# Decode attention: a group's scores behind the transposes of the next key page, with a ring of three PSUM banks

## The chip, the cores and the metric

One core of a Trainium2 chip runs the kernel once. The metric is the device time in microseconds of that one core. A profiled execution stands beside the timed runs; its rows are times from the start of its span.

## What is computed

One layer of a decoder for a prompt of 512 tokens and 8 requests ("sample group") of 4 new tokens each. The part at hand is the differential attention of the 8 requests over 1024 cached keys and values:

```python
s = jnp.einsum('bqhmd,bkhmd->bhmqk', q, k, preferred_element_type=jnp.float32) * (DA_HEAD_DIM ** -0.5)
...
s = jnp.where(causal, s + bias[:, None], -jnp.inf)
p = jax.nn.softmax(s, axis=-1)
a = p[:, :, 0] - lam * p[:, :, 1]
return jnp.einsum('bhqk,bkhd->bqhd', a, v)
```

There are 8 heads, two softmax maps per head and 4 queries, so 64 score rows for a request. Keys and values lie in a cache of pages of 128 keys, 512 KB each, found through a page table: 8 key pages and 8 value pages for a request. Feed-forward blocks, projections, the prompt's attention and a retention branch stand before and behind this stage and are not touched.

## The kernel before, in words

Each engine has its own program, and they meet at semaphores. All five programs of the stage are unrolled over requests b = 0 to 7 and pages g = 0 to 7 except SyncE's, which loops over the middle requests. `DecodeAttention` (from line 1140) holds them. Products are made in two parts: each float operand is split in a "high" part (a rounding copy to the matmul type) by ScalarE and a "low" part (source less high) by VectorE.

A key page lands in one of four slots of `k_page`. `turn` (line 1255) transposes it on TensorE in two halves of four heads: half 0 goes to PSUM bank 0 and half 1 to bank 1. Before each half it waits until the low part of the half two earlier is taken (`kT_lo`, line 1260). ScalarE's `act_key` writes the high half to `kt_hi`, VectorE's `dve_key` the low one to `kt_lo` (`key_half`, line 1374). `kt_hi` and `kt_lo` have two slots of two pages each, so ScalarE waits at an even page for the scores of the pair two earlier (`scored`, line 1386). `score_pair` (line 1266) multiplies two pages (a pair, q = 0 to 3) with the queries: one matmul for the bias and 16 for eight heads and two parts. It waits for both pages' low halves, for q = 0 also for the minimum taken of the request before (`s_min`) and the queries that GpSimd sets.

After the fourth pair of a request ScalarE copies the low score rows out (`act_low_rows`), VectorE adds the rest and takes the minimum (`dve_min`), ScalarE makes the exponential (`act_exp`), TensorE turns p (`turn_p`, line 1284, into bank 5), and ScalarE and VectorE split it (`act_p`, `dve_p`) into `pT`. Then the value pages: `act_value` and `dve_value` (lines 1395 and 1400) split a page into `vp_hi` and `vp_lo`, which have two slots, so page g waits for the matmuls of page g - 2 (`pv`). `values` (line 1298) makes four matmuls of a page into banks 6 and 7, and `values_new` (line 1309) adds the new tokens. ScalarE copies the output to `o_rows` (`act_keep`), VectorE prepares weights (`dve_weigh`), and `merge` (line 1315) makes 8 small fp32 matmuls (16 in the profile) out of it.

The order of the work is written out by hand, once for each engine: `pe_step` (line 1325), `act_step` (line 1447), `dve_step` (line 1534), and `sp_step` and `sp_ahead` (lines 1186 and 1200) for the loads on SyncE's queue. An engine takes its instructions in that order, and one that waits holds what is behind it. In the step of request b TensorE turns and scores the keys of b, multiplies the values of b - 1 (pages 0 to 5) and those of b - 2 (pages 6 and 7), and merges b - 2. Before, its order is: turn 0, values 6, turn 1, values 7 and new, turn 2, turn p, score 0, turn 3, values 0 and 1, score 1, merge, turn 4, values 2, turn 5, values 3, score 2, turn 6, values 4, turn 7, values 5, score 3. ScalarE and VectorE take value page g - 2 ahead of key page g for g = 4 to 7, and value pages 6 and 7 at the end of the step:

```python
for g in range(4, PAGES):
    if past:
        self.act_value(act, b - 1, g - 2)
    self.act_key(act, b, g)
```

A key page's load (`load_page`, line 1173) waits until the page four earlier is transposed, a value page's until the low part of the page four earlier is taken. Behind the last request a tail (lines 1359 to 1371) finishes the values of requests 6 and 7, with the first chunks of the next stage's gate between.

Of the kernel before, what the change touches and what calls it, by code (L numbers as in the profile page):

```python
# [15 lines left out]
P = 128  # L16
# [84 lines left out]
def build(nc, x_prompt, x_sample, cache_k, cache_v, state_ret, page_table, ln_g, ln_b, ffn1_w_gu,  # L101
# [6 lines left out]
    with ExitStack() as ctx:  # L108
# [1031 lines left out]
        class DecodeAttention:  # L1140
            def __init__(self):
# [29 lines left out]
                self.oa_set = sem("da_oa_set")  # L1171

# [13 lines left out]
            def sp_step(self, sp, b, older=True):  # L1186

                self.load_k(sp, b, 4)
                if older:
                    self.load_v(sp, b - 1, 2)  # L1190
                self.load_k(sp, b, 5)
                if older:
                    self.load_v(sp, b - 1, 3)
                self.load_k(sp, b, 6)
                self.load_k(sp, b, 7)
                if older:
                    self.load_v(sp, b - 1, 4)
                    self.load_v(sp, b - 1, 5)

            def sp_ahead(self, sp, b, older=True):  # L1200

                for g in range(2):
                    self.load_k(sp, b + 1, g)
                    if older:
                        self.load_v(sp, b - 1, 6 + g)
                for g in range(2):
                    self.load_k(sp, b + 1, 2 + g)
                    self.load_v(sp, b, g)

            def sp_part(self, sp):  # L1210
# [9 lines left out]
                self.sp_step(sp, DEC - 1)  # L1220
                self.load_v(sp, DEC - 2, 6)
# [33 lines left out]
            def turn(self, pe, b, g):  # L1255

                for half in range(2):
                    if half == 0:
                        pe.wait_ge(self.k_landed[g % 4], 32 * b + 16 * (g // 4) + 16)
                    pe.wait_ge(self.kT_lo, 16 * b + 2 * g + half + 1)  # L1260
                    for h in range(4):
                        mm = nc.tensor.transpose(ps[:, half, h * P:h * P + P],  # L1262
                                                 k_page[:, g % 4, (4 * half + h) * P:(4 * half + h) * P + P], ident[:])
# [20 lines left out]
            def turn_p(self, pe, b):  # L1284
                pe.wait_ge(self.exped, b + 1)
                pe.wait_ge(self.pT_lo, 2 * b + 2)

                nc.tensor.matmul(ps[:, 5, 0:ROWS], p_s[:, 0:P], ident[:, 0:ROWS], start=True, stop=True)
                for g in range(1, PAGES):
                    nc.tensor.transpose(ps[:, 5, ROWS * g:ROWS * g + ROWS], p_s[0:ROWS, P * g:P * g + P],  # L1290
# [34 lines left out]
            def pe_step(self, pe, b):  # L1325

                past, older = b >= 1, b >= 2
                self.turn(pe, b, 0)
                if older:
                    self.values(pe, b - 2, 6)  # L1330
# [5 lines left out]
                if past:  # L1336
                    self.turn_p(pe, b - 1)
                self.score_pair(pe, b, 0)
                self.turn(pe, b, 3)
                if past:  # L1340
                    self.values(pe, b - 1, 0)
                    self.values(pe, b - 1, 1)
                self.score_pair(pe, b, 1)
                if older:
                    self.merge(pe, b - 2)
                for q in (2, 3):
                    for g in (2 * q, 2 * q + 1):
                        self.turn(pe, b, g)
                        if past:
                            self.values(pe, b - 1, g - 2)  # L1350
                    self.score_pair(pe, b, q)

            def pe_part(self, pe):
# [3 lines left out]
                for b in range(DEC):  # L1357
                    self.pe_step(pe, b)
                self.values(pe, DEC - 2, 6)
# [14 lines left out]
            def key_half(self, b, g, half, hi):  # L1374
                src = ps[:, half, :].rearrange("p (h c) -> p h c", c=P)
# [29 lines left out]
            def p_parts(self):  # L1405

                return ((ps[:, 5, :].rearrange("p (g c) -> p g c", c=ROWS), pT[:, 0:PAGES, 0:ROWS],
# [28 lines left out]
            def act_p(self, act, b):  # L1436
                act.wait_ge(self.p_turned, b + 2)
                act.wait_ge(self.o_done, b + 1)
                for src, hi, _ in self.p_parts():
# [7 lines left out]
            def act_step(self, act, b):  # L1447
                past, older = b >= 1, b >= 2
                if past:
                    self.act_low_rows(act, b - 1)  # L1450
                self.act_key(act, b, 0)
                if past:
                    self.act_exp(act, b - 1)
                self.act_key(act, b, 1)
# [4 lines left out]
                self.act_key(act, b, 2)  # L1459
                if past:  # L1460
                    self.act_p(act, b - 1)
                    self.act_value(act, b - 1, 1)
                self.act_key(act, b, 3)
                for g in range(4, PAGES):
                    if past:
                        self.act_value(act, b - 1, g - 2)
                    self.act_key(act, b, g)
                if past:
                    self.act_value(act, b - 1, 6)
                    self.act_value(act, b - 1, 7)  # L1470

            def act_part(self, act):
                for b in range(DEC):
                    self.act_step(act, b)
                self.act_low_rows(act, DEC - 1)
                self.act_exp(act, DEC - 1)
# [41 lines left out]
            def dve_p(self, dve, b):  # L1518
                dve.wait_ge(self.pT_hi, 2 * b + 2)
                for src, hi, lo in self.p_parts():  # L1520
# [13 lines left out]
            def dve_step(self, dve, b):  # L1534
                past = b >= 1
                if past:
                    self.dve_min(dve, b - 1)
                self.dve_key(dve, b, 0)
                self.dve_key(dve, b, 1)
                if past:  # L1540
                    self.dve_value(dve, b - 1, 0)
                self.dve_key(dve, b, 2)
                if past:
                    self.dve_p(dve, b - 1)
                    self.dve_value(dve, b - 1, 1)
                self.dve_key(dve, b, 3)
                for g in range(4, PAGES):
                    if past:
                        self.dve_value(dve, b - 1, g - 2)
                    self.dve_key(dve, b, g)  # L1550
                    if past and g == 5:
                        self.dve_weigh(dve, b - 1)
                if past:
                    self.dve_value(dve, b - 1, 6)
                    self.dve_value(dve, b - 1, 7)

            def dve_part(self, dve):
                for b in range(DEC):
                    self.dve_step(dve, b)
                self.dve_min(dve, DEC - 1)  # L1560
                self.dve_value(dve, DEC - 1, 0)
# [656 lines left out]
```

## Time and profile before

| | us |
|---|---|
| median of 3 runs | 1928.66 |
| lowest, highest | 1927.82, 1928.72 |
| the profiled execution's own time | 1928.45 |
| its span | 1926.2 |
| TensorE busy in it | 1776.9 |
| VectorE, ScalarE busy in it | 780.3, 660.8 |
| first turn of the stage to its last merge | 736.23 to about 1020 |

PE is TensorE, PEld its weight loads, ACT ScalarE, DVE VectorE, POOL GpSimd and SPq SyncE's queue. A group of matmuls on one line is often folded into one row with its count (x8 is the eight transposes of one page). The span of 1926.2 us is what the rows cut up; the execution's own time lies 2.25 us over it. A number in square brackets is the idle time of the engine before the instruction, and what ended it.

### The profile page before, as it was taken

How to read it: one execution, taken by the hardware profiler on the slowest of the kernel's cores; microseconds unless marked ns; L12 is line 12 of the kernel's file. 1: busy time of each engine (PE TensorE's matmuls, PEld its weight loads, DVE VectorE, ACT ScalarE, POOL GpSimd, SP SyncE). 2: the span in 40 equal slices, each digit the busy share in tenths (PEclk: the TensorE clock that was granted, in tenths of full speed). 3: DMA queues.
4: the chain of work that ended last, by engine and by line, in shares of the span. 5: the costliest groups of instructions: out<-in, count | busy, mean ns of one | idle time of the engine just before them, and what ended most of it. 6: DMA issues, size and time to landing. Idle time of an engine off the chain costs nothing.

```text
span 1926.2 us, 32228 instructions
## 1 busy us (share of the span) xinstructions
PE 1776.9 (92%) x13095; PEld 1680.3 (87%) x13095; DVE 780.3 (41%) x1084; ACT 660.8 (34%) x867; POOL 97.1 (5%) x169
## 2 busy tenths in 40 slices
PE   5999999998998775889889999899999899999996
PEld 5999999987997545777778999769998899999996
DVE  2333332234223775676753222344345433333123
ACT  3333331124223554666744222124322433332111
POOL 0000000000002420000000000210000000000002
PEclk9999999998998898999979999999999999999998
DMA  4222222231431014788851232062222122222221
GB/s 140 88 87 87 87 87 98 82 92 39 134 122 36 1 34 145 260 279 276 274 186 44 87 100 88 31 199 72 95 87 97 37 88 89 89 88 84 84 98 46
DMA packets 146736, 204.12 MB, mean 106 GB/s; under 512 B 5538, under 2 KB 127330, under 8 KB 146658
## 3 DMA queue, kind: packets, MB, share of 16 engines
q1 hardware_dynamic: 145506, 198.55, 31.6%
q0 software_dynamic: 1152, 4.46, 0.6%
q8 instruction: 58, 0.95, 0.2%
q14 instruction: 20, 0.16, 0.0%
HBM read 191.59 MB, written 11.40 MB: 105 GB/s over the span
## 4 chain that ended last, share of the span: by engine, by line
PE 86%; DVE 6%; ACT 5%; issue 3%; DMA 0%; SPq 0%; POOL 0%; POOLq 0%; ACTq 0%; DVEq 0%
PE ps L297 68%; PE ps L1280 3%; PE ps L1305 2%; PE ps L1262 2%; PE ps L999 2%; DVE vp_lo L1402 2%; PE ps L311 1%; ACT vp_hi L1398 1%; PE ps L1013 1%; PE ps L636 1%; ACT kt_hi L1380 1%; PE ps L1708 1%; PE ps L1320 1%; PE ps L1700 1%; PE ps L721 1%
## 5 line engine op out<-in xcount | busy, mean ns | idle before, releaser
L297 PE MATMUL ps<-xh,w_hi_t 128*128 128x272 f32 x2368 | 495.8, 291 | 8.4 <-DVE xl L568 4.8
L297 PE MATMUL ps<-xl,w_hi_t 128*128 128x272 f32 x2368 | 491.9, 289 | 0.0
L297 PE MATMUL ps<-xh,w_lo_t 128*128 128x272 f32 x2368 | 490.6, 289 | 0.0
L283 DVE TENSOR_TENSOR w_lo_t<-w_raw,w_hi_t 128x2048 fp32r<-128x2048 f32 (+1 forms) x112 | 252.4, 2254 | 516.1 <-ACT w_hi_t L279 516.1
L297 PEld LDWEIGHTS ps<-xh,w_hi_t 128*128 128x128 f32 x2368 | 373.9, 190 | 10.7 <-issue 4.9
L297 PEld LDWEIGHTS ps<-xl,w_hi_t 128*128 128x128 f32 x2368 | 375.3, 190 | 0.0
L297 PEld LDWEIGHTS ps<-xh,w_lo_t 128*128 128x128 f32 x2368 | 373.2, 190 | 0.0
L279 ACT CAST w_hi_t<-w_raw 128x2048 fp32r<-128x2048 f32 (+1 forms) x112 | 209.9, 1874 | 277.1 <-PE ps L297 277.1
L297 PE MATMUL ps<-hh,w_hi_t 128*128 128x272 f32 x704 | 145.7, 288 | 0.0
L297 PE MATMUL ps<-hl,w_hi_t 128*128 128x272 f32 x704 | 145.4, 288 | 0.0
L297 PE MATMUL ps<-hh,w_lo_t 128*128 128x272 f32 x704 | 144.9, 287 | 0.0
L297 PEld LDWEIGHTS ps<-hl,w_hi_t 128*128 128x128 f32 x704 | 110.7, 189 | 0.0
L297 PEld LDWEIGHTS ps<-hh,w_hi_t 128*128 128x128 f32 x704 | 110.2, 188 | 0.0
L297 PEld LDWEIGHTS ps<-hh,w_lo_t 128*128 128x128 f32 x704 | 110.2, 188 | 0.0
L1381 DVE TENSOR_TENSOR kt_lo<-ps,kt_hi 128x512 fp32r<-128x512 f32 x128 | 82.6, 684 | 62.5 <-ACT kt_hi L1380 61.7
L399 ACT CAST hh<-prod 128x544 f32 x44 | 28.5, 648 | 214.8 <-DVE prod L416 214.8
L1380 ACT CAST kt_hi<-ps 128x512 fp32r<-128x512 f32 x128 | 70.1, 589 | 77.8 <-PE ps L1262 75.3
L1262 PE MATMUL ps<-ident,k_page 128*128 128x128 f32 x512 | 72.1, 284 | 20.5 <-DVE kt_lo L1381 18.1
L1262 PEld LDWEIGHTS ps<-ident,k_page 128*128 128x128 f32 x512 | 58.4, 145 | 33.8 <-issue 30.3
L1402 DVE TENSOR_TENSOR vp_lo<-v_page,vp_hi 128x1024 fp32r<-128x1024 f32 x64 | 78.2, 1223 | 21.0 <-ACT vp_hi L1398 17.9
L416 DVE TENSOR_TENSOR prod<-ps,gated 128x544 f32<-128x544 f32 x44 | 31.9, 725 | 107.0 <-PE ps L297 107.0
L1398 ACT CAST vp_hi<-v_page 128x1024 fp32r<-128x1024 f32 x64 | 67.3, 1053 | 20.1 <-PE ps L1305 20.1
(249 smaller groups left out, 2126.6 us busy)
## 6 DMA issues: line engine op xcount, KB each, us to landing
w_raw<-in_ffn_w_gu_dram SPq DMA_DIRECT2D x44, 1024.0 KB, 5.0
w_raw<-in_w_in_dram SPq DMA_DIRECT2D x32, 1024.0 KB, 5.7
k_page<-in_cache_k_dram SPq DMA_DIRECT2D x64, 512.0 KB, 4.3
v_page<-in_cache_v_dram SPq DMA_DIRECT2D x64, 512.0 KB, 4.6
w_raw<-in_ffn_w_down_dram SPq DMA_DIRECT2D x16, 1024.0 KB, 5.1
w_raw<-in_ffn_w_down_dram SPq DMA_DIRECT2D x8, 768.0 KB, 4.4
w_raw<-in_w_branch_a_dram SPq DMA_DIRECT2D x4, 1024.0 KB, 5.2
st_in<-in_state_ret_dram SPq DMA_DIRECT2D x8, 512.0 KB, 5.3
```

Of the source, the lines that this page charges most:

```text
L279: nc.scalar.copy(w_hi_t[:, j, 0:nk], w_raw[:, j, 0:nk]).then_inc(hi_split, 1)
L283: nc.vector.tensor_tensor(w_lo_t[:, j, 0:nk], w_raw[:, j, 0:nk], w_hi_t[:, j, 0:nk].bitcast(F32), ALU.subtract).then_inc(lo_split, 1)
L297: mm = nc.tensor.matmul(ps[:, bank + half, 0:HALF], w[:, j, k, w_cols], m[:, k0 + k, half * HALF:half * HALF + HALF], start=start and k == ...
L416: nc.vector.tensor_tensor(halves(prod[:, n]), banks(4 + 2 * n), halves(gated[:, n]), ALU.mult).then_inc(self.prod_done, 1)
L999: mm = nc.tensor.matmul(ps[:, 2 * s + m, 0:n], q_stage[:, s, m], kaT[:, h, 0:n], start=True, stop=True)
L1262: mm = nc.tensor.transpose(ps[:, half, h * P:h * P + P], k_page[:, g % 4, (4 * half + h) * P:(4 * half + h) * P + P], ident[:])
L1280: mm = nc.tensor.matmul(dst, q_stat[:, P * h:P * h + P], kt[:, q % 2, h, 0:n], start=False, stop=h == HA - 1 and kt is kt_lo)
L1305: mm = nc.tensor.matmul(ps[:, 6 + half, :], pT[:, g], v[:, g % 2, 512 * half:512 * half + 512], start=g == 0 and v is vp_hi, stop=False)
L1380: return nc.scalar.copy(at_hi, src)
L1381: return nc.vector.tensor_tensor(at_lo, src, at_hi.bitcast(F32), ALU.subtract)
L1398: nc.scalar.copy(vp_hi[:, g % 2], v_page[:, g % 4]).then_inc(self.v_hi, 1)
L1402: nc.vector.tensor_tensor(vp_lo[:, g % 2], v_page[:, g % 4], vp_hi[:, g % 2].bitcast(F32), ALU.subtract).then_inc(self.v_lo, 1)
```

## The change

Three things go together. The halves of the keys and the turned p share a ring of three banks (0, 1 and 5), in an order listed once, and each waits for the item three earlier. On TensorE a pair's scores move behind the first turn of the next pair, so score 3 of a request stands behind turn 0 of the next; turning p moves behind turn 3, the merge behind that, and the values are dealt out anew. ScalarE, VectorE and SyncE get new orders to go with it: value pages 6 and 7 move into the next step, the copy of the output (`act_keep`) behind key 3, and from key 4 on each value page stands behind a key page. The diff, cut to its core:

```diff
+                order = []
+                for b in range(DEC):
+                    for g in range(PAGES):
+                        order += [("k", b, g, half) for half in range(2)]
+                        if b and g == 3:
+                            order.append(("p", b - 1))
+                order.append(("p", DEC - 1))
...
+            def bank(self, *item):
+                return (0, 1, 5)[self.place[item] % 3]
+            def bank_free(self, pe, *item):
+                n = self.place[item] - 3
+                if n >= 0 and self.order[n][0] == "k":
+                    _, b, g, half = self.order[n]
+                    pe.wait_ge(self.kT_lo, 16 * b + 2 * g + half + 3)
+                elif n >= 0:
+                    pe.wait_ge(self.pT_lo, 2 * self.order[n][1] + 3)
...
 sp_step: the load of value 5 leaves it; sp_ahead becomes
+                self.load_k(sp, b + 1, 0)
+                if older:
                     self.load_v(sp, b - 1, 5)
+                self.load_k(sp, b + 1, 1)
+                if older:
+                    self.load_v(sp, b - 1, 6)
+                self.load_k(sp, b + 1, 2)
+                if older:
+                    self.load_v(sp, b - 1, 7)
+                self.load_k(sp, b + 1, 3)
                 for g in range(2):
                     self.load_v(sp, b, g)
...
 turn:
-                    pe.wait_ge(self.kT_lo, 16 * b + 2 * g + half + 1)
+                    self.bank_free(pe, "k", b, g, half)
...
 pe_step:
                 self.turn(pe, b, 0)
+                if past:
+                    self.score_pair(pe, b - 1, 3)
                 if older:
                     self.values(pe, b - 2, 6)
                 self.turn(pe, b, 1)
...
                 self.turn(pe, b, 2)
-                if past:
-                    self.turn_p(pe, b - 1)
                 self.score_pair(pe, b, 0)
                 self.turn(pe, b, 3)
                 if past:
-                    self.values(pe, b - 1, 0)
-                    self.values(pe, b - 1, 1)
-                self.score_pair(pe, b, 1)
+                    self.turn_p(pe, b - 1)
                 if older:
                     self.merge(pe, b - 2)
-                for q in (2, 3):
-                    for g in (2 * q, 2 * q + 1):
-                        self.turn(pe, b, g)
-                        if past:
-                            self.values(pe, b - 1, g - 2)
-                    self.score_pair(pe, b, q)
+                self.turn(pe, b, 4)
+                self.score_pair(pe, b, 1)
+                if past:
+                    self.values(pe, b - 1, 0)
+                self.turn(pe, b, 5)
+                if past:
+                    self.values(pe, b - 1, 1)
+                    self.values(pe, b - 1, 2)
+                self.turn(pe, b, 6)
+                self.score_pair(pe, b, 2)
+                if past:
+                    self.values(pe, b - 1, 3)
+                self.turn(pe, b, 7)
+                if past:
+                    self.values(pe, b - 1, 4)
+                    self.values(pe, b - 1, 5)
...
 act_step after the change (dve_step has the same order, with dve_min in the
 place of act_low_rows, and dve_weigh between key 6 and value 3):
+                if older:
+                    self.act_value(act, b - 2, 6)
+                self.act_key(act, b, 0)
                 if past:
                     self.act_low_rows(act, b - 1)
+                if older:
+                    self.act_value(act, b - 2, 7)
+                self.act_key(act, b, 1)
                 if past:
                     self.act_exp(act, b - 1)
+                self.act_key(act, b, 2)
+                self.act_key(act, b, 3)
                 if past:
                     self.act_value(act, b - 1, 0)
                 if older:
                     self.act_keep(act, b - 2)
                 if past:
                     self.act_p(act, b - 1)
+                self.act_key(act, b, 4)
+                if past:
                     self.act_value(act, b - 1, 1)
+                self.act_key(act, b, 5)
+                if past:
+                    self.act_value(act, b - 1, 2)
+                self.act_key(act, b, 6)
+                if past:
+                    self.act_value(act, b - 1, 3)
+                self.act_key(act, b, 7)
+                if past:
+                    self.act_value(act, b - 1, 4)
+                    self.act_value(act, b - 1, 5)
```

In the tail TensorE begins with score 3 of request 7, and ScalarE and VectorE take value 6 of request 6 ahead of the score rows (the minimum on VectorE) and value 7 behind them; SyncE loads value 5 of request 6 there as well.

## Rows read from the trace of the kernel before

**Rows 1.** The page, busy time and share of TensorE over the span.
```profile
PE 1776.9 (92%) x13095; PEld 1680.3 (87%) x13095; DVE 780.3 (41%) x1084; ACT 660.8 (34%) x867; POOL 97.1 (5%) x169
```

**Rows 2.** Two stretches: length, busy PE, PEld, DVE, ACT, POOL, clock, DMA share, GB/s.
```profile
736.00:768.00 32.00, 21.95 (x140) 19.73 (x140) 11.65 (x18) 11.04 (x20) 2.15 (x11) 0.84 0.52 165
...
864.00:896.00 32.00, 28.94 (x201) 24.47 (x200) 23.31 (x34) 21.52 (x33) 1.36 (x7) 1.00 0.81 277
```

**Rows 3.** TensorE's timeline, steady request: start us, length us, instruction, [idle before <-releaser].
```profile
835.32 0.33 PE L1288 MATMUL ps<-ident,p_s 128*128 128x64 f32 x2
...
836.21 0.39 PE L1277 MATMUL ps<-bias_r,ident_r 128*128 128x256 f32 x1
...
838.31 1.04 PE L1262 MATMUL ps<-ident,k_page 128*128 128x128 f32 x8
...
839.11 0.48 PE L1305 MATMUL ps<-vp_hi,pT 128*128 128x512 f32 x1
...
841.04 0.28 PE L1277 MATMUL ps<-bias_r,ident_r 128*128 128x256 f32 x1
...
843.06 1.84 PE L1320 MATMUL ps<-weights,o_rows 128*128 128x4 f32 x16
...
844.76 1.07 PE L1262 MATMUL ps<-ident,k_page 128*128 128x128 f32 x8
...
848.82 0.50 PE L1305 MATMUL ps<-vp_hi,pT 128*128 128x512 f32 x1 [0.71 <-DVE vp_lo L1402]
```

**Rows 4.** TensorE's timeline, behind the last score groups of requests 1 and 7.
```profile
798.20 1.03 PE L1262 MATMUL ps<-ident,k_page 128*128 128x128 f32 x8
...
982.01 0.39 PE L1305 MATMUL ps<-vp_hi,pT 128*128 128x512 f32 x1
...
985.82 0.43 PE L1288 MATMUL ps<-ident,p_s 128*128 128x64 f32 x2 [1.36 <-ACT p_s L1433]
```

**Rows 5.** The waits of the stage: total us, times, longest.
```profile
PE ps L1262 <- DVE kt_lo L1381: 18.1, 26, 2.2
```

**Rows 6.** ScalarE's timeline: the kept output, a key and a value page, the score rows.
```profile
834.69 1.02 ACT L1445 COPY o_rows<-ps 128x1024 f32<-128x1024 f32 x1
...
845.49 1.07 ACT L1380 CAST kt_hi<-ps 128x512 fp32r<-128x512 f32 x2 [4.06 <-PE ps L1262]
...
846.45 1.06 ACT L1398 CAST vp_hi<-v_page 128x1024 fp32r<-128x1024 f32 x1
...
982.21 1.02 ACT L1429 COPY p_s<-ps 64x1028 f32<-64x1028 f32 x1 [1.20 <-PE ps L1280]
```

**Rows 7.** VectorE's timeline: key and value low halves, weighing, the minimum.
```profile
846.10 1.29 DVE L1381 TENSOR_TENSOR kt_lo<-ps,kt_hi 128x512 fp32r<-128x512 f32 x2 [3.42 <-ACT kt_hi L1380]
...
847.54 1.23 DVE L1402 TENSOR_TENSOR vp_lo<-v_page,vp_hi 128x1024 fp32r<-128x1024 f32 x1
...
849.88 0.14 DVE L1526 RECIPROCAL small<-small 64x1 f32<-64x1 f32 x1
...
850.39 1.22 DVE L1402 TENSOR_TENSOR vp_lo<-v_page,vp_hi 128x1024 fp32r<-128x1024 f32 x1
...
983.26 1.22 DVE L1515 CUSTOM_DVE_ANT_0 p_s<-ps,p_s 64x1028 f32<-64x1028 f32 x1 [1.00 <-issue]
```

**Rows 8.** TensorE's timeline of request 0.
```profile
742.57 0.56 PE L1277 MATMUL ps<-bias_r,ident_r 128*128 128x256 f32 x1
...
755.12 0.58 PE L1277 MATMUL ps<-bias_r,ident_r 128*128 128x256 f32 x1 [1.47 <-DVE kt_lo L1381]
...
758.67 1.04 PE L1262 MATMUL ps<-ident,k_page 128*128 128x128 f32 x8
...
765.60 1.03 PE L1262 MATMUL ps<-ident,k_page 128*128 128x128 f32 x8
```

**Rows 9.** TensorE's timeline in request 1.
```profile
771.80 1.77 PE L1262 MATMUL ps<-ident,k_page 128*128 128x128 f32 x8 [1.82 <-DVE kt_lo L1381]
...
778.66 1.13 PE L1262 MATMUL ps<-ident,k_page 128*128 128x128 f32 x8
```

More of the change, by code:

```diff
@@ L1171, in __init__ @@
                 self.oa_set = sem("da_oa_set")
+                order = []
[5 more added lines that the diff above has]
+                order.append(("p", DEC - 1))
+                self.order = order
+                self.place = {item: n for n, item in enumerate(order)}
+            def bank(self, *item):
[7 more added lines that the diff above has]
+                    pe.wait_ge(self.pT_lo, 2 * self.order[n][1] + 3)
             def load_page(self, sp, cache, ring, landed, free, steps, b, g):
@@ L1286, in turn_p @@
                 pe.wait_ge(self.pT_lo, 2 * b + 2)
-                nc.tensor.matmul(ps[:, 5, 0:ROWS], p_s[:, 0:P], ident[:, 0:ROWS], start=True, stop=True)
+                self.bank_free(pe, "p", b)
+                bank = self.bank("p", b)
+                nc.tensor.matmul(ps[:, bank, 0:ROWS], p_s[:, 0:P], ident[:, 0:ROWS], start=True, stop=True)
                 for g in range(1, PAGES):
-                    nc.tensor.transpose(ps[:, 5, ROWS * g:ROWS * g + ROWS], p_s[0:ROWS, P * g:P * g + P],
+                    nc.tensor.transpose(ps[:, bank, ROWS * g:ROWS * g + ROWS], p_s[0:ROWS, P * g:P * g + P],
                                         ident[0:ROWS, 0:ROWS])
@@ L1374, in key_half @@
             def key_half(self, b, g, half, hi):
-                src = ps[:, half, :].rearrange("p (h c) -> p h c", c=P)
+                src = ps[:, self.bank("k", b, g, half), :].rearrange("p (h c) -> p h c", c=P)
                 n = slice(P * (g % 2), P * (g % 2) + P)
@@ L1534, in dve_step @@
             def dve_step(self, dve, b):
-                past = b >= 1
+                past, older = b >= 1, b >= 2
+                if older:
+                    self.dve_value(dve, b - 2, 6)
+                self.dve_key(dve, b, 0)
                 if past:
                     self.dve_min(dve, b - 1)
-                self.dve_key(dve, b, 0)
+                if older:
+                    self.dve_value(dve, b - 2, 7)
                 self.dve_key(dve, b, 1)
+                self.dve_key(dve, b, 2)
+                self.dve_key(dve, b, 3)
                 if past:
                     self.dve_value(dve, b - 1, 0)
-                self.dve_key(dve, b, 2)
+                    self.dve_p(dve, b - 1)
+                self.dve_key(dve, b, 4)
                 if past:
-                    self.dve_p(dve, b - 1)
                     self.dve_value(dve, b - 1, 1)
[L1546 to L1552, printed above, removed]
-                if past:
-                    self.dve_value(dve, b - 1, 6)
-                    self.dve_value(dve, b - 1, 7)
+                self.dve_key(dve, b, 5)
+                if past:
+                    self.dve_value(dve, b - 1, 2)
+                self.dve_key(dve, b, 6)
+                if past:
+                    self.dve_weigh(dve, b - 1)
+                    self.dve_value(dve, b - 1, 3)
+                self.dve_key(dve, b, 7)
+                if past:
+                    self.dve_value(dve, b - 1, 4)
+                    self.dve_value(dve, b - 1, 5)
             def dve_part(self, dve):
```

33 lines of the change are left out of this document (12 added, 21 removed).

## The prediction

> **What bounds the kernel now.** I read the page first: TensorE is busy for 92% of the span [rows 1], so the path that sets the end runs through it, and a change inside one stage counts by what it adds to or takes from TensorE's time there. The change touches only decode attention, from 736 to about 1016 us. The table by stretches shows the stage [rows 2]: from 864 to 896 us TensorE is busy for 28.94 of 32 us at full clock (1.00, the 2.4 GHz level) while VectorE has 23.31 and ScalarE 21.52; the DMA share is 0.81. In the first stretch the mean clock was 0.84. So TensorE leads with neither helper full: what it loses are waits for them.
>
> The third view is TensorE's timeline of one request in the steady part [rows 3]. Start to start, undisturbed: a page's eight transposes ("turn") 0.80 us (838.31 to 839.11); the turning of p 0.89 (835.32 to 836.21); a score group 2.10 (836.21 to 838.31); two value groups 1.93 (839.11 to 841.04), so 1.0 for a single one and 0.24 for a matmul; a merge 1.70 (843.06 to 844.76). A request needs 8 x 0.80 + 0.89 + 4 x 2.10 + 8 x 1.0 + 0.48 (new values) + 1.70 = 25.9 us. The last score group of request 1 ends at 798.20 and that of request 7 at 982.01 [rows 4], so six requests took 183.8 us, 30.63 each. 4.7 us of each is waiting. The list of waits names the cause the change aims at: TensorE waited 18.1 us for the key low halves before turns [rows 5], that is for one of two banks to be free; other waits stand before scores and values.
>
> **The change, part by part.** The arithmetic, the instruction counts and the DMA bytes stay the same. What moves is who stands behind whom in three in-order queues, and a bank is reused after three half pages instead of two. Call S the end of a request's last score group.
>
> *The key chain* (what a third bank buys). A page's transposes are followed by the high half on ScalarE and the low half on VectorE. The fourth key page of the steady request shows it with what follows: turn at 844.76, high halves from 845.49 [rows 6], then the value page's high half, its low half from 847.54 to 848.77 [rows 7], and its matmuls at 848.82 [rows 3]. Two numbers come from it: a value page whose halves stand behind a key page's in both helper queues is ready 4.06 us after that key page's turn began; and the key page itself is ready 2.6 us after its turn began (VectorE's two low halves end at 846.10 + 1.29 [rows 7]).
>
> *Request 0* has only turns and scores. Today its last score group ends at 765.60 [rows 8]. After: the score of a pair starts 2.6 us after the pair's second turn began, and that turn starts where the score before ends, because the pair's first turn already stands ahead of it. A pair costs 2.1 + 2.6 = 4.7 us. The first score starts at 742.57 now; with three banks two waits before the third turn go, and I put it at 740.9. It runs at the low clock, like most of today's (3.55 us for such a group, 755.12 to 758.67 [rows 8]): 744.5, then 747.1, 751.8, 756.5 are the starts of the others, and S is 758.6. That is -7.0 us.
>
> *A steady request, value pages 2 to 5.* This is where I expect the loss. The new TensorE order is turn 5, values 1, values 2, turn 6, score 2, values 3, turn 7, values 4, values 5; ScalarE and VectorE take key 5, value 2, key 6, value 3, key 7, value 4, value 5. Before, each value page's halves stood behind the key page *one turn earlier*, so the 4.06 us ran beside a whole turn and a value group, and only 0.71 was left [rows 3]. Now they stand behind the key page just turned.
> - Values 2: ready 4.06 after turn 5 began; TensorE has 0.8 + 1.0 to do. Wait 2.2.
> - Values 3: ready at 4.06 plus the three small weighing operations, which now stand ahead of it (849.88 to 850.39, so 0.51, less overlap: 4.3 [rows 7]); TensorE has 0.8 + 2.1. Wait 1.4.
> - Values 4: ready 4.06 after turn 7; TensorE has 0.8. Wait 3.2. Values 5 adds 0.2, since VectorE needs 1.23 for its half and TensorE 1.0.
>
> *The merge* now follows turn 3 and the turning of p. It waits for the copy that keeps the output, and ScalarE has key 3 and value 0 ahead of that. Turn 3 begins; 0.7 later key 3, 0.96 later (845.49 to 846.45) value 0, about as much later the copy, 1.02 long [rows 6]: 3.6 in all, against 0.8 + 0.9 of work. Wait 1.9 (behind it are queued turn 4 and score 1).
>
> *Values 7* stands on VectorE behind the minimum, which needs the score rows. From S: ScalarE's copy starts 0.20 later (982.21 [rows 6]), the minimum 1.25 after S (983.26 to 984.48 [rows 7]), so the low half runs from 2.4 to 3.65 after S. TensorE has values 6 and turn 1, 1.8. Wait 1.9. Everything else (score 0, key 1, turn 2) comes in time behind it.
>
> *Sum.* Waits of 2.2 + 1.4 + 3.2 + 0.2 + 1.9 + 1.9 = 10.8, with 25.9 of work 36.7; following the order with its overlaps gives 36.9. That is +6.3 a request over 30.63, and 6 x 6.3 = +37.6. Request 1 has no merge and no values 6 and 7; the same walk gives 31.65 from S to S (turn 5 begins 12.1 after S, then 5.05, 5.33 and 9.17), against 32.6 now (798.20 less 765.60): -0.95. After request 7 no turn stands ahead of its last score: -0.8. The tail starts with values 7 behind the minimum, so the turning of p begins 5.15 after S instead of 3.81 (985.82 [rows 4]), but the copies behind it absorb part: +0.9. At full clock: -7.0 - 0.95 + 37.6 - 0.8 + 0.9 = +29.8 us.
>
> *SyncE's queue.* Pages are issued in another order: value 5, 6 and 7 now stand behind keys 0, 1 and 2 of the next request, and value 0 behind key 3. Each key load still waits for the turn of the page four earlier. A page needs under 5 us; the tightest, value 0, is issued about 4 us after turn 7 and used 12 after it. I cost this at nothing; the cover is the slower step. If a request did come down to 26 us, this cover would go: the DMA share of 0.81 over 30.63 us [rows 2] is 24.8 us of transfers.
>
> *The clock.* The rows show what waits do. After a wait of 1.82 us the turn at 771.80 and the two groups behind it, to 778.66, took 6.86 us where 3.79 is normal: a spell at the low level (0.5, 1.2 GHz) cost 3.07 [rows 9]. The spell at 755.12 cost 3.55 - 2.10 = 1.45 [rows 8], after a similar mix of turns and waits. In the steady part, whose 4.7 us of waits come in smaller pieces, there was none [rows 2]. The new request has 6.2 us from score 0 to score 1 with only transposes, a merge and a wait, and a 3.2 us wait behind turn 7. Bounds: none (0), or two long spells in each of seven requests (7 x 6.1 = +43). I take one spell in each at the mean of the two seen, 2.3 us: +16, nearest to requests 0 and 1, whose busy share is like the new one's.
>
> The Trainium skill, "TensorE: Matmul & The Clock Gate", section "A second HAM failure mode: psum-queue depth-cycling", says that cycling through PSUM banks with short idle times between groups can make the clock go up and down and cost throughput even so. By that rule the third bank itself could bring spells; the steady part, which cycles through two banks with short idles at 1.00, does not bear that out, and by the row the spells come with longer waits.
>
> Total: 1928.45 (the profiled execution; its span is 1926.2, and the median of the runs is 1928.66) + 29.8 + 16 = **1974 us**, or +45 on the median.
>
> **Rivals.** (a) *Faster: the banks were the limit.* If ScalarE and VectorE did the value halves ahead of need, a request would be TensorE's own 25.9: 6 x (25.9 - 30.63) - 7 - 1 = -36, so 1892 us. For it speak the 18.1 us [rows 5]. It decides at the place of value 2 to 4 in ScalarE's queue: were they issued before keys 5 to 7, it holds; the diff issues them after. The Trainium skill, "Perfetto Trace Analysis", section "Optimization Strategy", says that a gap that repeats on the engine that should be saturated can mean too few buffers in SBUF or PSUM; that rule would stand behind this case. Chance 0.04.
> (b) *The change does not do what it says: waits only trade places.* If the new waits equal the old 4.7 us, only requests 0 and 1 gain: 1920 to 1930 us. Against it, 3.2 us behind turn 7 alone uses most of that. Chance 0.04, half of it within 0.2%.
> (c) *Slower still by the clock.* Two long spells a request: 1928.45 + 29.8 + 43 = 2001 us. For it, the low stretch at the start; against it, that scores and values still fill most of a request. Chance 0.10.
>
> **How the numbers follow.** My forecast has 0.82. A measurement of this kernel can tell about 0.2%, 4 us, from no change. Within the forecast the clock term runs from 0 to about 30 and the walk may be off by 1 us a request, so 1953 to 1990; the range goes on to 1998 for part of (c). Slower: 0.82 + 0.10 = 0.92; the same: 0.02; faster: 0.04 + 0.02 = 0.06.
>
> **What would show it.** The last score groups of requests 1 and 7 should lie about 220 us apart at full clock, 230 or more with spells, against 183.8. The timeline should have a wait of about 3.2 us for the value low half behind turn 7, 2.2 behind values 1, 1.9 for the kept output before the merge and 1.9 before values 7; waits for key low halves should nearly vanish, and S of request 0 should come near 758.6. If the waits behind turn 5 and turn 7 are under 1 us, I am wrong in the queues; if they are there and the clock stays at 1.00, the time is near 1958 and only the clock term fails.

## The result and the profile after

The changed kernel takes 1976.38 us (median of four runs, 1972.49 to 1988.26) against 1928.69 (1927.82 to 1928.87): a ratio of 1.0259, 95% interval 1.0214 to 1.0303. The forecast was 1974. The profiled execution took 1972.49 with a span of 1970.2, the fastest of the four, and its page answers to [rows 1] so:

```profile
span 1970.2 us, 32226 instructions
PE 1787.2 (91%) x13095; PEld 1695.9 (86%) x13095; DVE 781.9 (40%) x1084; ACT 659.2 (33%) x867; POOL 97.2 (5%) x169
```

The counts of instructions are those of before, and so is the busy time of the helpers (VectorE 781.9 against 780.3). TensorE is busy 10 us longer with the same matmuls, while the span is 44.0 us longer. So the time came mostly as waits, and for a smaller part as slower matmuls. What stands behind the stage's last merge takes 906.5 us (1970.2 less 1063.72) against 907.9 before: the time came inside the stage.

The waits of the whole stage, its tail included (waiter, releaser: us in total, times, longest), to be held against [rows 5]:

```profile
PE ps L1334 <- DVE vp_lo L1440: 54.1, 28, 2.9
...
PE ps L1349 <- ACT o_rows L1483: 11.8, 7, 1.8
...
PE ps L1289 <- DVE kt_lo L1419: 3.8, 5, 1.7
```

The waits for a free key bank went from 18.1 to 3.8 us, which is what the third bank was put there for (e3 below shows that TensorE's new order had the larger part in it). In their place TensorE waits 54.1 us for value low halves and 11.8 for the output copy. In the same stretch of the kernel before these are:

```profile
PE ps L1305 <- DVE vp_lo L1402: 12.3, 16, 1.5
...
PE ps L1320 <- ACT o_rows L1445: 1.1, 1, 1.1
```

One steady request in TensorE's timeline, from the merge of the request two before to value page 7, as [rows 3]:

```profile
838.68 0.22 PE L1323 MATMUL ps<-ident,p_strip 64*64 64x64 f32 x1
...
840.68 1.95 PE L1349 MATMUL ps<-weights,o_rows 128*128 128x4 f32 x16 [1.78 <-ACT o_rows L1483]
...
851.83 0.50 PE L1334 MATMUL ps<-vp_hi,pT 128*128 128x512 f32 x1 [2.01 <-DVE vp_lo L1440]
...
857.17 0.50 PE L1334 MATMUL ps<-vp_hi,pT 128*128 128x512 f32 x1 [1.28 <-DVE vp_lo L1440]
...
858.21 1.04 PE L1289 MATMUL ps<-ident,k_page 128*128 128x128 f32 x8
...
862.17 0.50 PE L1334 MATMUL ps<-vp_hi,pT 128*128 128x512 f32 x1 [2.93 <-DVE vp_lo L1440]
...
867.25 0.39 PE L1334 MATMUL ps<-vp_hi,pT 128*128 128x512 f32 x1
...
870.92 0.50 PE L1334 MATMUL ps<-vp_hi,pT 128*128 128x512 f32 x1 [1.71 <-DVE vp_lo L1440]
```

Five waits at the five places of the forecast: 1.78, 2.01, 1.28, 2.93 and 1.71 us by the brackets, where it had 1.9, 2.2, 1.4, 3.2 and 1.9 (the two don't count from the same point; see the account below). The helpers' timelines show why the largest is there. The turn of key page 7 begins at 858.21; ScalarE, then VectorE:

```profile
858.84 1.07 ACT L1418 CAST kt_hi<-ps 128x512 fp32r<-128x512 f32 x2 [3.26 <-PE ps L1289]
859.80 2.00 ACT L1436 CAST vp_hi<-v_page 128x1024 fp32r<-128x1024 f32 x2
```

```profile
859.46 1.29 DVE L1419 TENSOR_TENSOR kt_lo<-ps,kt_hi 128x512 fp32r<-128x512 f32 x2 [2.34 <-ACT kt_hi L1418]
860.89 2.36 DVE L1440 TENSOR_TENSOR vp_lo<-v_page,vp_hi 128x1024 fp32r<-128x1024 f32 x2
```

ScalarE stood idle for 3.26 us ahead of the key half, until TensorE had turned the page, with two value pages landed and waiting behind it in its queue. Value 4 is ready 3.96 us after the turn began (862.17 less 858.21; [rows 3, 7] gave 4.06).

The clock, by stretches of the request before that one (length, busy times by engine, granted clock, DMA share, GB/s):

```profile
794.80:802.30 7.50, 5.72 (x54) 5.49 (x53) 4.62 (x7) 4.47 (x8) 0.00 (x0) 1.00 0.66 212
802.30:806.80 4.50, 4.50 (x27) 4.50 (x27) 2.60 (x3) 2.12 (x3) 0.00 (x0) 0.62 0.64 214
806.80:812.70 5.90, 3.90 (x22) 2.97 (x21) 2.53 (x4) 2.02 (x3) 0.00 (x0) 1.00 0.60 187
812.70:817.50 4.80, 4.66 (x26) 4.43 (x24) 2.96 (x6) 2.12 (x3) 0.00 (x0) 0.64 0.67 207
817.50:822.50 5.00, 2.09 (x12) 1.61 (x12) 2.50 (x5) 2.96 (x4) 0.00 (x0) 1.00 0.64 202
822.50:826.00 3.50, 3.42 (x10) 2.56 (x11) 1.74 (x3) 1.04 (x1) 0.00 (x0) 0.58 0.71 219
```

Three spells with the clock at the low level in one request: behind the merge that waited for the output copy, behind the wait before values 2, and behind that before values 4. A stretch whose mean lies between 0.50 and 1.00 is partly at either level. [rows 2] have 1.00 for 32 us of the steady part of before.

The end of a request's last score group is read as the start of the instruction behind it: 756.49 (request 0), 788.85, 829.03, 867.25, 907.35, 945.57, 985.66 and 1026.73 (request 7). Of these:

```profile
788.85 0.39 PE L1334 MATMUL ps<-vp_hi,pT 128*128 128x512 f32 x1
...
985.66 0.40 PE L1334 MATMUL ps<-vp_hi,pT 128*128 128x512 f32 x1
...
1026.73 0.39 PE L1334 MATMUL ps<-vp_hi,pT 128*128 128x512 f32 x1
```

From request 1 to 7 it is 237.9 us against 183.8 [rows 4].

### The profile page after: what moved, and what is told of

It reads as the page before. It is cut to its first block, busy times and chain, and to the rows that moved or that the text cites. A ratio compares the mean times of both kernels' runs of the same rounds, so it can differ in the third digit from the quotient of the medians.

```text
span 1970.2 us, 32226 instructions
## 1 busy us (share of the span) xinstructions
PE 1787.2 (91%) x13095; PEld 1695.9 (86%) x13095; DVE 781.9 (40%) x1084; ACT 659.2 (33%) x867; POOL 97.2 (5%) x169
## 4 chain that ended last, share of the span: by engine, by line
PE 84%; DVE 7%; ACT 5%; issue 3%; DMA 0%; SPq 0%; POOL 0%; POOLq 0%; ACTq 0%; DVEq 0%
PE ps L297 66%; PE ps L1334 3%; PE ps L1307 2%; PE ps L1289 2%; DVE vp_lo L1440 2%; PE ps L999 2%; PE ps L311 1%; ACT vp_hi L1436 1%; ACT kt_hi L1418 1%; PE ps L1013 1%; PE ps L636 1%; PE ps L1349 1%; DVE kt_lo L1419 1%; PE ps L1766 1%; PE ps L1758 1%
## 5 line engine op out<-in xcount | busy, mean ns | idle before, releaser
L1334 PE MATMUL ps<-vp_hi,pT 128*128 128x512 f32 x128 | 60.8, 475 | 55.8 <-DVE vp_lo L1440 54.1
L1334 PEld LDWEIGHTS ps<-vp_hi,pT 128*128 128x128 f32 x128 | 27.1, 212 | 71.1 <-DVE vp_lo L1440 65.5
L1289 PEld LDWEIGHTS ps<-ident,k_page 128*128 128x128 f32 x512 | 64.7, 152 | 14.1 <-DVE kt_lo L1419 5.0
```

The source lines that it names most:

```text
L1289: mm = nc.tensor.transpose(ps[:, self.bank("k", b, g, half), h * P:h * P + P], k_page[:, g % 4, (4 * half + h) * P:(4 * half + h) * P + P] ...
L1334: mm = nc.tensor.matmul(ps[:, 6 + half, :], pT[:, g], v[:, g % 2, 512 * half:512 * half + 512], start=g == 0 and v is vp_hi, stop=False)
```

## The experiments

Theory: the loss is made of helper operations that stand too late in a helper's queue, behind key halves that wait for TensorE, and of low-clock spells that these waits bring. Rivals: the third bank or the late scores cost the time; the clock is no price of its own; the helpers or the loads would bound a request in any order. The kernel before, timed beside the experiments, took 1928.43 us beside the first four and 1928.17 beside the rest. Each edit is made in the changed kernel unless it says otherwise.

**Value pages ahead of key pages (e1).** ScalarE's part of the edit; VectorE has the same.

```diff
                 self.act_key(act, b, 4)
                 if past:
                     self.act_value(act, b - 1, 1)
+                    self.act_value(act, b - 1, 2)
                 self.act_key(act, b, 5)
                 if past:
-                    self.act_value(act, b - 1, 2)
+                    self.act_value(act, b - 1, 3)
                 self.act_key(act, b, 6)
                 if past:
-                    self.act_value(act, b - 1, 3)
-                self.act_key(act, b, 7)
-                if past:
                     self.act_value(act, b - 1, 4)
                     self.act_value(act, b - 1, 5)
+                self.act_key(act, b, 7)
```

> The changed kernel with one edit: on ScalarE and VectorE the halves of value pages 2, 3, 4 and 5 stand ahead of key pages 5, 6 and 7 again (value 1, value 2, key 5, value 3, key 6, weighing, value 4, value 5, key 7). TensorE's order and the three banks stay. Theory (the value halves behind the key halves cost the time): the waits before values 2, 3 and 4 go from 2.0, 1.3 and 2.9 us to about 0.85, 0 and 0, with about 0.85 before values 5; a steady request comes down by 5 us or more, from 39.5 to 33 or 34; in all 1976 becomes 1935 to 1945, the waits before the merge and values 7 (1.8 and 1.7) are still there. Rival (the ring of three banks or the order of the scores costs the time): still 1970 or more.

Measured: 1931.02 us (1927.37 to 1938.26), a ratio of 1.0019 (1.0001 to 1.0038) to before: by the medians 45 us of the loss are gone by an edit of two helper orders, and the time lies 4 us below the lowest that was expected. In the profiled executions the stage, from its first turn to its last merge, takes 287.8 us against 327.7 of the changed kernel (282.1 before), so 40 us less; the profiled execution of the changed kernel was the fastest of its runs. The list of waits:

```profile
PE ps L1334 <- DVE vp_lo L1440: 24.5, 24, 2.6
...
PE ps L1349 <- ACT o_rows L1483: 11.8, 7, 1.8
```

Value waits fell from 54.1 to 24.5 us, and 0.65 is left before values 2 and before values 5, where 0.85 was expected; the merge's wait stayed at 11.8, as it should. A request takes 33.9 us (six in 203.3). The banks and TensorE's order, late scores included, were in it unchanged, so by themselves they are not what cost 45 us.

**The output copy earlier (e2).**

```diff
                 if past:
                     self.act_exp(act, b - 1)
+                if older:
+                    self.act_keep(act, b - 2)
                 self.act_key(act, b, 2)
                 self.act_key(act, b, 3)
                 if past:
                     self.act_value(act, b - 1, 0)
-                if older:
-                    self.act_keep(act, b - 2)
```

> The changed kernel with one edit: ScalarE's copy of the output stands behind the exponential, ahead of keys 2 and 3 and value 0. Theory (the merge waits for that copy, and the long stretch without scores or values lowers the clock): the wait of 1.8 us before the merge goes in six requests, -11 us, and part of the low-clock spells in that stretch with it, -5: about 1960. Rival (the merge's wait covers work that is late anyway, so the wait moves on to turn 4 or score 1): 1972 or more.

Measured: 1954.48 us (1952.04 to 1961.42), 22 below the changed kernel where 16 were expected. The merge no longer waits. Successive requests take 36.74, 34.88, 36.68, 34.86 and 36.66 us, so one without spells takes 34.9, which is 1.8 less than the 36.7 below: the wait itself. From request 1 to 7 it is 217.6 us against 237.9, 20.3 less: 10.8 of them are six waits of 1.8, and the other 9.5 are clock, where I had counted 5. Every second request now has no spell at all: the two of 34.9 us are at 1.00 throughout.

**Two key banks again (e3).**

```diff
             def bank(self, *item):
-                return (0, 1, 5)[self.place[item] % 3]
+                return 5 if item[0] == "p" else item[3]
             def bank_free(self, pe, *item):
...
+                if item[0] == "k":
+                    _, b, g, half = item
+                    pe.wait_ge(self.kT_lo, 16 * b + 2 * g + half + 1)
```

> The changed kernel with one edit: the key halves use two banks again (0 and 1, each waiting for the half two earlier), the turned p bank 5; all orders stay as changed. Theory (the banks are not what the steady requests wait for): steady requests stay at 38 to 40 us, only request 0 and the first half of request 1 lose about 0.5 us a pair, so 1976 to 1985. Rival (the third bank itself, by cycling or by what it lets go ahead, made the kernel slower): the time falls by 10 us or more.

Measured: 1982.18 us (1981.59 to 1982.6). Its median is 6 us higher, but the runs of the changed kernel reach from 1972.49 to 1988.26, so the times alone don't settle whether the third bank is a gain; they do settle that taking it away is not the gain of 10 us or more that the rival wanted. The timelines show where the bank counts. Request 0 takes 24.6 us against 20.4 from its first turn (a pair 5.1 against 4.7, and its first score group at the low clock), and request 1 34.6 against 32.4. Requests 2 to 7 take 40.25 us each, against 39.65, and all of that stands in request 3, which takes 41.95 us against 38.22; the others are alike within 0.1. The list of waits has

```profile
PE ps L1286 <- DVE kt_lo L1416: 7.4, 7, 2.2
```

So with two banks and TensorE's new order the waits for a key bank are already 7.4 us where they were 18.1: most of that fall is the order's, and the third bank takes it from 7.4 to 3.8.

**Waits filled with matmuls (e4).** The added matmuls are work that the kernel doesn't need, and their results are overwritten.

```diff
+            def fill(self, pe, n, bank, at):
+                for _ in range(n):
+                    nc.tensor.matmul(ps[:, bank, at:at + 256], ident_r[:], bias_r[:, 0:256], start=True, stop=True)
...
                 if older:
+                    self.fill(pe, 12, 3, 0)
                     self.merge(pe, b - 2)
...
                     self.values(pe, b - 1, 1)
+                    self.fill(pe, 14, 3, 256)
                     self.values(pe, b - 1, 2)
...
                 if past:
+                    self.fill(pe, 22, 4, 0)
                     self.values(pe, b - 1, 4)
```

> The changed kernel with extra matmuls in three of TensorE's waits, in every request from 1 on (merge: from 2 on): 12 ahead of the merge, 14 ahead of values 2, 22 ahead of values 4, each 128x256 like the bias matmul, into score banks that are free there; their result is overwritten. They fit in the waits (about 0.115 us each). Theory (low-clock spells cost about 16 to 19 us beside the waits): the granted clock stays at 1.00 through the steady requests, these take 36.7 us each, and the time comes to about 1955, with less spread between runs. Rival (the clock is not a price of its own): 1972 or more, since waits are all there and work is added.

Measured: 1958.86 us (1957.74 to 1959.8), 4 above what was expected: a kernel with 48 more matmuls in each steady request is 17.5 us faster. The waits are the same (what was idle is filled, and 0.31 us is left before values 4). TensorE's clock in a steady stretch, and the turns of key page 3 in four successive requests:

```profile
832.00:864.00 32.00, 28.74 (x213) 25.79 (x211) 19.15 (x28) 17.55 (x26) 1.18 (x6) 1.00 0.70 222
```

```profile
795.50 1.04 PE L1289 MATMUL ps<-ident,k_page 128*128 128x128 f32 x8
...
832.23 1.04 PE L1289 MATMUL ps<-ident,k_page 128*128 128x128 f32 x8
...
868.90 1.04 PE L1289 MATMUL ps<-ident,k_page 128*128 128x128 f32 x8
...
905.60 1.04 PE L1289 MATMUL ps<-ident,k_page 128*128 128x128 f32 x8
```

They lie 36.73, 36.67 and 36.70 us apart: this is the changed order at full clock, and the walk had 36.9. It is not at full clock everywhere: request 5 takes 38.24 us, with a mean clock of 0.72 from 909 to 915, behind a merge whose wait is filled, and request 7 has a spell as well (0.83 from 988 to 994). So the spells cost about 17.5 us beside the waits, and a little more if those that are left are counted. The runs lie within 2.1 us where those of the changed kernel lie within 15.8; but those of e3, whose requests have the same spells, lie within 1.0, so the spread isn't shown to come from them.

**Every late operation earlier (e5).** TensorE's order and the ring stay; ScalarE and VectorE take, from the top of the step: value 6, key 0, value 7, score rows or minimum, key 1, exponential, output copy, key 2, value 0, key 3, p, key 4, value 1, value 2, key 5, value 3, key 6, weighing, value 4, value 5, key 7.

```diff
                 self.act_key(act, b, 0)
+                if older:
+                    self.act_value(act, b - 2, 7)
                 if past:
                     self.act_low_rows(act, b - 1)
-                if older:
-                    self.act_value(act, b - 2, 7)
...
                 self.act_key(act, b, 2)
+                if past:
+                    self.act_value(act, b - 1, 0)
                 self.act_key(act, b, 3)
-                if past:
-                    self.act_value(act, b - 1, 0)
```

> The changed kernel with new orders on ScalarE and VectorE alone: value pages 2 to 5 ahead of key pages (as in the first experiment), the output copy behind the exponential (as in the second), value 0 ahead of key 3, and value 7 ahead of the score rows and the minimum. TensorE's order and the three banks stay. Theory (every wait of the changed kernel is one of a half or a copy standing too late in a helper's queue): the waits before the merge and values 7 go, about 0.65 us stay before values 2 and before values 5; a steady request takes 27.5 to 28.5 us against 30.63 of the kernel before and the clock stays at 1.00; request 0 ends 9 to 11 us earlier than before; in all 1893 to 1902, faster than both kernels. Rival (the loads or the helpers' own sum then bound a request): 30 us a request or more, 1912 or more.

Measured: 1896.16 us (1894.53 to 1900.86), a ratio of 0.9841 (0.9825 to 0.9858) to before: faster than both kernels. From its timeline, ends of last score groups with the wait that is left before values 2 (another of 0.65 stands before values 5), and a stretch with the clock:

```profile
808.68 0.39 PE L1334 MATMUL ps<-vp_hi,pT 128*128 128x512 f32 x1
...
824.78 0.50 PE L1334 MATMUL ps<-vp_hi,pT 128*128 128x512 f32 x1 [0.65 <-DVE vp_lo L1440]
...
836.20 0.39 PE L1334 MATMUL ps<-vp_hi,pT 128*128 128x512 f32 x1
```

```profile
832.00:864.00 32.00, 30.45 (x223) 27.54 (x224) 26.11 (x39) 22.73 (x35) 2.10 (x8) 1.00 0.88 303
```

A request takes 27.52 us, of which 1.3 are waits, against 30.63 before and 36.7 at full clock with the changed helper orders. VectorE is at 26.11 of 32 us, ScalarE at 22.73, the DMA share at 0.88, and no engine waits for a landed page: none of them bounds yet. One request is an exception and takes 29.03 us. Behind turn 3, the turning of p and a merge that waited for nothing its score group ran at the low level:

```profile
899.34 1.95 PE L1349 MATMUL ps<-weights,o_rows 128*128 128x4 f32 x16
901.15 1.23 PE L1289 MATMUL ps<-ident,k_page 128*128 128x128 f32 x8
902.03 0.56 PE L1304 MATMUL ps<-bias_r,ident_r 128*128 128x256 f32 x1
...
905.61 0.40 PE L1334 MATMUL ps<-vp_hi,pT 128*128 128x512 f32 x1
```

The group takes 3.58 us where 2.1 is usual. A spell can thus come behind transposes and a merge without a wait. What the four moves of this edit bring singly was run for the first two alone (e1, e2).

**The same with two banks (e6).** The edit of e3 in the kernel of e5.

> The kernel of the run before it with two key banks again and the turned p in bank 5. It prices the third bank where little else waits. Theory: request 0 ends 3 us later (759.5 against 756.4 in the third experiment) and steady requests lose 0 to 0.5 us each, so 3 to 6 us over the run before it. Rival (without a third bank a group's scores can't stand behind the next turn at this pace, since a half's low part comes too late): 1.5 us a request or more, 12 us over it or more.

Measured: 1905.16 us (1904.4 to 1905.92), 9 us slower than e5, which is between the theory's 3 to 6 and the rival's 12. From the last score group of request 0 to that of 7 it is 3.1 us longer (0.45 a request), as expected, and request 0 takes 3.5 us longer. From first turn to last merge the stage takes 256.8 us against 250.7. The remainder lies ahead of the stage: its first turn began at 738.70 in the profiled execution against 733.42, by nothing that this edit touches. That start lies anywhere from 733.4 to 738.7 in the ten traces, and a median of four runs carries some of it.

**Values dealt anew on TensorE (e7).** In the kernel of e5 (behind the last request values 5 of request 6 are added likewise):

```diff
                 self.turn(pe, b, 0)
+                if older:
+                    self.values(pe, b - 2, 5)
...
                     self.values(pe, b - 1, 1)
-                    self.values(pe, b - 1, 2)
                 self.turn(pe, b, 6)
+                if past:
+                    self.values(pe, b - 1, 2)
...
                     self.values(pe, b - 1, 4)
-                    self.values(pe, b - 1, 5)
```

> The kernel of run e5 with TensorE's values 2 moved behind turn 6 and values 5 behind the next turn 0, so that each of the two has a turn more ahead of it. Theory: the two waits of about 0.65 us go, a steady request comes to 26.5 to 27.3 us, near TensorE's own 25.9, and the time falls 5 to 8 us below e5. Rival (the DMA queue, 24.8 us of transfers a request by the share of before, gives late pages at that pace): no more than 2 us below e5, with waits for landed pages on ScalarE.

Measured: 1902.86 us (1896.33 to 1909.6), not faster than e5. Both expectations fail: nothing is gained, and no engine waits for a landed page. The wait moved by one place:

```profile
829.21 0.66 PE L1289 MATMUL ps<-ident,k_page 128*128 128x128 f32 x4 [0.82 <-DVE kt_lo L1422]
829.62 0.47 PE L1334 MATMUL ps<-vp_hi,pT 128*128 128x512 f32 x1
```

The second half of turn 6 comes so soon after turn 5 that its bank isn't free: value 2 stands ahead of key 5 on VectorE. A request takes 27.7 us against 27.5. That makes 1 to 2 us in all. The rest of the 6.7 us between the two medians is not the edit's, as far as the profiled executions show: e7's, its slowest run at 1909.6 us, is 15.1 us longer in span than e5's, and of these 4.0 lie ahead of the stage, 0.8 in it (251.5 against 250.7 us) and 10.3 behind it, in the same work at a lower mean clock (0.96 against 0.97).

**The ring alone (e8).** The kernel before, with the ring of three banks and no order changed (in the ring p stands behind key page 2, since TensorE turns it there).

> The kernel before with the ring of three banks alone (turned p behind key page 2 in it); every order stays as before. It prices the one part of the change that takes a wait away. Theory: request 0 gains 0.8 us a pair (3 us), the wait of 1.26 us before turn 1 shrinks by 0.4 or more in each steady request while the value waits of 0.7 us stay or grow: 1918 to 1926. Rival (those waits were the bound): 2.5 us a request or more, 1910 or less. Another rival (the third bank costs by itself): over 1928.

Measured: 1919.69 us (1918.27 to 1921.33), a ratio of 0.9956 (0.9939 to 0.9972). From its timeline:

```profile
821.99 1.04 PE L1284 MATMUL ps<-ident,k_page 128*128 128x128 f32 x8
...
837.39 1.07 PE L1284 MATMUL ps<-ident,k_page 128*128 128x128 f32 x8
...
841.44 0.50 PE L1329 MATMUL ps<-vp_hi,pT 128*128 128x512 f32 x1 [1.18 <-DVE vp_lo L1426]
...
852.12 1.03 PE L1284 MATMUL ps<-ident,k_page 128*128 128x128 f32 x8
...
855.25 0.66 PE L1284 MATMUL ps<-ident,k_page 128*128 128x128 f32 x4 [0.73 <-DVE kt_lo L1405]
```

A steady request takes 30.13 us, 0.5 less than before. The wait before turn 1 fell from 1.27 to 0.73, and there the request gains. The short wait before turn 5 (0.18) is gone too, but the value wait behind it grew from 0.71 [rows 3] to 1.18: TensorE arrives 0.47 earlier at the same value half, and from turn 4 to values 2 it is 4.05 us (837.39 to 841.44) where it was 4.06. This is the first part of the change, and it is a gain, of 8.5 us by the medians; 4.5 us of it are in request 0 (24.9 us against 29.4 from its first turn) and 3.15 in the six steady requests.

## Why the prediction was right

The bound was right: TensorE's waits made the time, and each wait stood where the walk had put it. By its terms:

| term | forecast | measured |
|---|---|---|
| end of request 0 | 758.6 | 756.49 |
| request 1 | 31.65 at full clock | 32.36 with spells, 31.24 at full clock (e4) |
| steady request at full clock | 36.9 | 36.7 (e4) |
| waits: merge, values 2, 3, 4, 7 | 1.9, 2.2, 1.4, 3.2, 1.9 | 1.92, 2.17, 1.39, 3.16, 1.87, counted as in the forecast |
| end of request 7 over before | about +45 | +44.7 |
| clock spells, in all | 16 (0 to 43) | about 17.5 (medians, e4), 19.5 (profiled execution) |
| sum | 1974 | 1976.4 |

*The total is better than its terms.* Split at full clock and clock, the profiled execution has: request 0 -9.1 (forecast -7.0), request 1 -1.4 (-0.95), the six behind it 6 x 36.7, less 0.7 since no turn stands ahead of the last score (e5's last request is that much shorter), against 183.8: +35.7 (+36.8), the tail +0.7 (+0.9). That is +25.9 where the forecast had +29.8. The clock brought 237.9 - 219.5 = 18.4 and 1.1 in request 1, 19.5 in all, where it had 16. So 3.9 us too much and 3.5 too little cancelled: that request 7 ended 44.7 us late, where about 45 was forecast, is partly luck.

*Request 0* came out 2 us better. The step had its first score group at the low clock, as before; in the trace it ran at full clock (742.33 less 740.22, the start of the group, is 2.11 us). What kept the spell away there wasn't tried.

*The value pages* were the main term. Moving their halves alone gave back 45 us by the medians (e1), 40 in the profiled executions, where the value waits fell by 29.6 us; spells went with them. Against 4.06 us taken from the old trace, the chain took 3.96. The brackets lie below every forecast wait because they count from the modelled end of the instruction before (a turn is 1.03 or 1.04 us long), and the forecast from where the next could start (0.80). Counted its way, values 4 began 3.16 us later than TensorE could have (862.17 - 858.21 - 0.80), and the five waits are those of the table: none is off by more than 0.04.

*The merge* was right in place and size, and e2 took it away. I had left open how the clock divides over the waits; e2's profiled execution puts on this one, in the longest stretch without scores or values, about as much again in lost clock (9.5 us over six requests). The wait is not all of it, since e4 and e5 each have a spell behind a merge without it.

*The clock term* was nearly right in sum but by rough means, so in part by luck: it had one spell of 2.3 us in each of seven requests. The requests alternate instead: those of 38.22 us have one of about 1.5 over the 36.7, those of 40.1 have two or three for 3.4. The average of 39.4 over the first five is 2.7 above 36.7. The psum-queue depth-cycling section of the Trainium skill's "TensorE: Matmul & The Clock Gate", which ties a varying clock to the cycling through banks with short idles, is not borne out as the cause here: e5 cycles through the same three banks, waits 0.65 us twice a request, and has 1.00 in all its steady requests but one. Nor is it the third bank: with two banks for the keys (e3) the spells of the changed order are there as well.

*The rivals.* Rival (a), that the banks were the limit, named the deciding place rightly: with the halves issued ahead of need (e5) a request falls to 27.5 us and the kernel to 1896, near the 1892 worked out there. Its premise doesn't hold, though: with two banks the same orders give 1905 (e6), so of the 32 us below the kernel before, 23 come from the orders and 9 at most from the bank (6 in the stage of the profiled executions), and the bank in the old orders gives 8.5 (e8). Whether better helper orders would do as much with TensorE's old order wasn't run. Rival (c) had the mechanism at over twice its size, 43 us against 17.5 to 19.5. *The loads* cost nothing, as costed: no engine waits for a landed page in the changed kernel.

## What to carry to other kernels

In an engine's queue, an operation whose input is long there must not stand behind one that waits for the busiest engine: look for idle time of a helper directly ahead of a pair of instructions, and ask which of the two could have gone first. A new buffer can move a wait to the next thing that is late (e8: the wait between turns only became a longer one before values; the 0.5 us a request were gained at turn 1). The orders were worth more than the buffer (e6 against e5). And price waits of TensorE of 2 or 3 us above their own length: here the clock that went with them cost 17.5 us or more.

## What the runs showed of the hardware that I had not expected

Work that nobody needs made a kernel faster: 48 extra matmuls a request in TensorE's waits held its clock at 1.00 but for two spells in requests 2 to 7 and took 17.5 us off (e4).

A wait isn't needed for a spell. In e5 the clock fell to the low level once in the steady part, behind turn 3, the turning of p and a merge, without a wait.

The spread of a kernel's runs goes with the mean clock. The four runs of the changed kernel took 1972.49, 1974.82, 1977.93 and 1988.26 us with mean granted clocks of 0.955, 0.954, 0.950 and 0.943, while those of the kernel before lie within 1.05 us. That spells in this stage make the spread isn't shown: e3 has them and lies within 1.0 us, and in e7 most of what its profiled run took over e5's came from a lower clock behind the stage. Why neighbouring requests of the same order alternate between 38.2 and 40.1 us wasn't tried.
